# Three row norms moved into the projections behind them, and the adding of expert results joined to one of them

## The reference

```python
def rms_norm(x, g):
    xf = x.astype(jnp.float32)
    y = xf * lax.rsqrt(jnp.mean(xf * xf, axis=-1, keepdims=True) + EPS)
    return (y * g.astype(jnp.float32)).astype(x.dtype)
...
        h = rms_norm(x, attn_norm_g[l])
        proj = jnp.matmul(h, w_in[l])
...
    y = jnp.zeros_like(hf).at[row_tok].add(yb.reshape(n_rows, D))
...
        h = _rmsnorm(x, norm_mix_pre[l]).astype(dt)
        z = h @ w_in[l]
...
        h = _rmsnorm(x, norm_ffn_pre[l]).astype(dt)
        gate, up = jnp.split(h @ ffn_w_up[l], 2, axis=-1)
        gate = _causal_dwconv(gate, ffn_conv_w[l], ffn_conv_b[l])
```

## Time and profile before

| what | us |
|---|---|
| median of 3 runs | 3374.01 (3365.13 to 3382.85) |
| the profiled execution, its own time | 3364.43 |
| its span on the core | 3362.7 |
| TensorE busy | 2846.3 (85% of the span) |
| VectorE busy | 1820.1 (54%) |
| ScalarE busy | 1352.1 (40%) |
| GpSimd busy | 352.3 (10%) |
| mean granted TensorE clock | 0.908 of full speed |

### The profile page before, as it was taken

How to read it: one execution, slowest core, us unless ns; L and a number is a source line. 1 busy time by engine, 2 the same in 40 slices (tenths; PEclk the granted TensorE clock), 3 DMA queues, 4 the chain that set the end, 5 groups by cost and what they waited for, 6 DMA issues and landing times. The chain is left out here.

```text
span 3362.7 us, 43086 instructions
## 1 busy us (share of the span) xinstructions
PE 2846.3 (85%) x14395; PEld 2341.1 (70%) x14395; DVE 1820.1 (54%) x2202; ACT 1352.1 (40%) x2006; POOL 352.3 (10%) x247
## 2 busy tenths in 40 slices
PE   3999987799559999993799978178976999999997
PEld 2788776687448888882677776066855788887876
DVE  2796417663459999995262444754345233332344
ACT  3222427612248888883222133345334222222232
POOL 0222210020021111111122100001000000000000
PEclk8999998899779999996899978598677999999999
DMA  2112225132189999994212210301121211111122
GB/s 83 35 49 74 81 78 186 44 107 100 65 295 412 412 412 412 412 404 187 57 54 79 70 32 2 113 14 42 22 91 66 63 50 44 49 44 37 50 103 78
DMA packets 253206, 420.94 MB, mean 125 GB/s; under 512 B 40141, under 2 KB 157956, under 8 KB 253092
## 3 DMA queue, kind: packets, MB, share of 16 engines
q1 hardware_dynamic: 217204, 349.83, 29.2%
q10 hardware_dynamic: 26496, 39.62, 3.2%
q0 software_dynamic: 9392, 29.99, 2.6%
HBM read 349.01 MB, written 70.36 MB: 125 GB/s over the span
## 5 line engine op out<-in xcount | busy, mean ns | idle before, releaser
L1870 DVE TENSOR_TENSOR e_w_lo<-e_ring,e_w_hi 128x1024 fp32r<-128x1024 f32 x384 | 446.5, 1217 | 47.8 <-ACT e_w_hi L1797 47.8
L1797 ACT CAST e_w_hi<-e_ring 128x1024 fp32r<-128x1024 f32 x384 | 377.6, 1049 | 38.1 <-PE banks L1727 30.3
L2199 PE MATMUL banks<-h_hi,u_w_hi 128*128 128x512 f32 x704 | 274.8, 390 | 10.4 <-DVE u_w_lo L2233 10.4
L2200 PE MATMUL banks<-h_lo,u_w_hi 128*128 128x512 f32 x704 | 274.6, 390 | 0.0
L2201 PE MATMUL banks<-h_hi,u_w_lo 128*128 128x512 f32 x704 | 274.5, 390 | 0.0
L1725 PE MATMUL banks<-e_w_hi,e_xT_hi 128*128 128x512 f32 x512 | 202.8, 396 | 0.0
L1727 PE MATMUL banks<-e_w_hi,e_xT_lo 128*128 128x512 f32 x512 | 200.0, 391 | 0.0
L1726 PE MATMUL banks<-e_w_lo,e_xT_hi 128*128 128x512 f32 x512 | 199.6, 390 | 0.0
L713 DVE SCALAR_TENSOR_TENSOR conv<-x_first,vectors,conv 128x1024 f32<-128x1024 f32 x120 | 187.7, 1564 | 9.0
L563 PE MATMUL banks<-h_hi,p_w_hi 128*128 128x512 f32 x384 | 155.0, 404 | 11.8 <-POOL p_w_lo L698 11.8
L2199 PEld LDWEIGHTS banks<-h_hi,u_w_hi 128*128 128x128 f32 x704 | 132.7, 188 | 38.3 <-issue 10.8
(11 more groups left out here) (548 smaller groups left out, 6359.5 us busy)
## 6 DMA issues: line engine op xcount, KB each, us to landing
e_ring<-in_w_gate_e_dram SPq DMA_DIRECT2D x128, 512.0 KB, 8.8
e_ring<-in_w_up_e_dram SPq DMA_DIRECT2D x128, 512.0 KB, 10.6
e_ring<-in_w_down_e_dram SPq DMA_DIRECT2D x128, 512.0 KB, 8.0
yT<-in_ffn_w_up_dram SPq DMA_DIRECT2D x44, 512.0 KB, 3.9
expert_results<-nothing SPq DMA_DIRECT2D x1, 16384.0 KB, 50.3
expert_results<-e_y ACTq DMA_DIRECT2D x32, 512.0 KB, 7.9
p_w<-in_w_in_dram SPq DMA_DIRECT2D x24, 512.0 KB, 3.9
fd_w<-in_ffn_w_down_dram SPq DMA_DIRECT2D x44, 256.0 KB, 2.7
```

Source lines behind the costliest of these rows:

```text
L1797: nc.scalar.copy(w_hi[:, part, :], experts.ring[:, slot, :]).then_inc(w_rounded, 1)
L1870: tt(w_lo[:, part, :], experts.ring[:, slot, :], w_hi[:, part, :].bitcast(F32), ALU.subtract).then_inc(w_split, 1)
L2199: nc.tensor.matmul(bank, w_hi[:, up, k, :], h_hi[:, k, tokens], start=(k == 0), stop=False)
L2200: nc.tensor.matmul(bank, w_hi[:, up, k, :], h_lo[:, k, tokens], start=False, stop=False)
```

## The change

Each of the three norms now runs inside the block of the projection that reads it, as `RowNorm` (n1, n4) or `CombinedNorm` (n3).

- Every engine's program of the projection starts with the norm's part. SP loads the weights of units 0 and 1 at once; `fill` of units 0 and 1 stands between the steps of the norm on ScalarE, and in `ffn_up` the rest of the weights between those on VectorE.
- `first_units` on TensorE: turn tiles 0 to 5; when tiles 0 to 3 have their rest (`parted`), multiply half 0 of unit 0 and of unit 1, with the turning of tile 6 after 3 feature slices and of tile 7 after 6; when all tiles have their rest, half 1 of unit 0 and of unit 1. The order is unit 0 half 0, unit 1 half 0, unit 0 half 1, unit 1 half 1; before it was both halves of unit 0 and then those of unit 1.
- In `ffn_up`, `projected` is raised by 2 after all four quarters; before it was raised by 1 after each unit.
- The squares, root and reciprocal of n1 move into `load_vectors`, tile by tile as x lands.
- The gathers, the adding, the squares and the storing of x (now 8 DMAs, one a tile) move into `project_columns`. Root and reciprocal are formed for two tiles at a time. The gathers have four tile slots (in `z_rwkv`) where they had eight. The recycling and the small block with the table now come ahead of the gathers.
- `zm`, `values` and `mlstm_o` lie in the place of `x`; no DMA or operation is added by that.

The diff, cut to its core:

```diff
--- before.py
+++ after.py
@@ -216,7 +219,11 @@
             dve.drain()
             nc.vector.tensor_reduce(dots[:], prod[:], AX, ALU.add).then_inc(lam_dot, 1)
             dve.wait_ge(lam_exp, 1)
+            dve.wait_ge(squared, 1)
+            nc.vector.tensor_scalar(ss[:], ss[:], 1.0 / D, EPS, ALU.mult, ALU.add).then_inc(meaned, 1)
             nc.vector.tensor_scalar(K.lam[:], exps[:, 1:2], exps[:, 0:1], -LAM_INIT, ALU.subtract, ALU.add)
+            dve.wait_ge(rooted, 1)
+            nc.vector.reciprocal(ss[:], ss[:])
...
+            for t in range(NT):
+                act.wait_ge(x_landed[t // 4], 16)
+                nc.scalar.activation(junk[:], x[:, t, :], ACT.Square, accum_out=ss[:, t:t + 1])
+                act.drain()
             act.wait_ge(lam_dot, 1)
             nc.scalar.activation(exps[:], dots[:], ACT.Exp).then_inc(lam_exp, 1)
-    return x_landed
+            act.sem_inc(squared, 1)
+            act.wait_ge(meaned, 1)
+            nc.scalar.activation(ss[:], ss[:], ACT.Sqrt).then_inc(rooted, 1)
...
+class RowNorm:
...
+    def scale(self, act, t):
+        if t >= 2:
+            act.wait_ge(self.turned, t - 1)
+        self.K.nc.scalar.activation(self.xn[:, t % 2, :], self.x[:, t, :], ACT.Copy, scale=self.rstd[:, t:t + 1]).then_inc(self.scaled, 1)
+
+    def round_off(self, act, t):
+        act.wait_ge(self.gained, t + 1)
+        self.K.nc.scalar.activation(self.hi[:, :, t * P:(t + 1) * P], self.whole[:, t % 2], ACT.Copy).then_inc(self.rounded, 1)
+
+    def turn(self, pe, t):
+        b = t % 2
+        pe.wait_ge(self.scaled, t + 1)
+        if t >= 2:
+            pe.wait_ge(self.gained, t - 1)
+        for k in range(KT):
+            mm = self.K.nc.tensor.transpose(self.K.ps[:, 4 + 2 * b + k // 4, (k % 4) * P:(k % 4 + 1) * P],
+                                            self.xn[:, b, k * P:(k + 1) * P], self.K.const("ident"))
+        mm.then_inc(self.turned, 1)
...
+    def on_scalar(self, act, between={}):
+        self.scale(act, 0)
+        self.scale(act, 1)
+        for t in range(NT):
+            self.round_off(act, t)
+            if t + 2 < NT:
+                self.scale(act, t + 2)
+            if t in between:
+                between[t]()
...
+    def on_vector(self, dve, between={}):
+        self.times_gain(dve, 0)
+        for t in range(NT):
+            if t + 1 < NT:
+                self.times_gain(dve, t + 1)
+            self.rest(dve, t)
+            if t in between:
+                between[t]()
+
+    def first_units(self, pe, split, banks, w_hi, w_lo, projected):
+
+        mm = self.K.nc.tensor.matmul
+        for t in range(NT - 2):
+            self.turn(pe, t)
+        for h in range(2):
+            pe.wait_ge(self.parted, NT // 2 * (h + 1))
+            for u in range(2):
+                if h == 0:
+                    pe.wait_ge(split, u + 1)
+                bank, tokens = banks(u, h), slice(h * HALF, (h + 1) * HALF)
+                for k in range(KT):
+                    mm(bank, w_hi(u, k), self.hi[:, k, tokens], start=(k == 0), stop=False)
+                    mm(bank, w_hi(u, k), self.lo[:, k, tokens], start=False, stop=False)
+                    last = mm(bank, w_lo(u, k), self.hi[:, k, tokens], start=False, stop=(k == KT - 1))
+                    if h == 0 and u == 0 and k in (2, 5):
+                        self.turn(pe, NT - 2 + (k == 5))
+                last.then_inc(projected, 1)
...
+class CombinedNorm(RowNorm):
...
+    def on_gpsimd(self, pool):
+        for t in range(NT):
+            if t >= self.SLOTS:
+                pool.wait_ge(self.added, t - self.SLOTS + 1)
+            for c in range(2):
+                pool.indirect_dma_start(self.y[:, t % self.SLOTS, c, :], None, self.results,
+                                        bass.IndirectOffsetOnAxis(ap=self.dest[:, 2 * t + c:2 * t + c + 1], axis=0)) \
+                    .then_inc(self.gathered[t], 16)
+
+    def on_sync(self, sp):
+        for t in range(NT):
+            sp.wait_ge(self.added, t + 1)
+            sp.dma_start(self.keep[t * P:(t + 1) * P, :], self.x[:, t, :]).then_inc(self.x_kept, 16)
+
+    def on_scalar(self, act, between={}):
+        for q in range(NT // 2):
+            for t in (2 * q, 2 * q + 1):
+                act.wait_ge(self.added, t + 1)
+                self.K.nc.scalar.activation(self.junk, self.x[:, t, :], ACT.Square, accum_out=self.rstd[:, t:t + 1])
+                act.drain()
+            act.sem_inc(self.squared, 1)
+            if q:
+                self.round_off(act, 2 * q - 2)
+            act.wait_ge(self.meaned, q + 1)
+            self.K.nc.scalar.activation(self.rstd[:, 2 * q:2 * q + 2], self.rstd[:, 2 * q:2 * q + 2], ACT.Sqrt).then_inc(self.rooted, 1)
+            if q:
+                self.round_off(act, 2 * q - 1)
+            act.wait_ge(self.rated, q + 1)
+            self.scale(act, 2 * q)
+            self.scale(act, 2 * q + 1)
+            if q in between:
+                between[q]()
+        self.round_off(act, NT - 2)
+        self.round_off(act, NT - 1)
+
+    def add(self, dve, t):
+        dve.wait_ge(self.gathered[t], 32)
+        for c in range(2):
+            last = self.K.nc.vector.scalar_tensor_tensor(self.x[:, t, :], self.y[:, t % self.SLOTS, c, :], self.weights[:, t, c:c + 1],
+                                                         self.x[:, t, :], ALU.mult, ALU.add)
+            if c == 0:
+                dve.drain()
+        last.then_inc(self.added, 1)
...
+    def on_vector(self, dve):
+        self.add(dve, 0)
+        self.add(dve, 1)
+        self.add(dve, 2)
+        self.mean(dve, 0)
+        self.add(dve, 3)
+        self.rate(dve, 0)
+        for q in range(NT // 2):
+            t = 2 * q
+            more = t + 4 < NT
+            if more:
+                self.add(dve, t + 4)
+            if t + 2 < NT:
+                self.mean(dve, q + 1)
+            self.times_gain(dve, t)
+            self.times_gain(dve, t + 1)
+            self.rest(dve, t)
+            if more:
+                self.add(dve, t + 5)
+            if t + 2 < NT:
+                self.rate(dve, q + 1)
+            self.rest(dve, t + 1)
+        dve.wait_ge(self.x_kept, 16 * NT)
...
+            norm.on_sync(sp)
...
+            norm.first_units(pe, split, lambda u, h: K.ps[:, 2 * u + h, :], lambda u, k: w_hi[:, u, k * P:(k + 1) * P],
+                             lambda u, k: w_lo[:, u, k * P:(k + 1) * P], projected)
+            for u in range(2, U):
                 b = u % 2
                 pe.wait_ge(split, u + 1)
                 for h in range(2):
-                    pe.wait_ge(kept, 2 * u + h + 1)
+                    pe.wait_ge(kept, 2 * u + h + (2 if u == 2 and h else 1))
...
-            fill(0)
-            fill(1)
+            norm.on_scalar(act, {1: lambda: fill(0), 2: lambda: fill(1)})
+            for n, (u, h) in enumerate([(0, 0), (1, 0), (0, 1), (1, 1)]):
+                _, out, scale, func, _ = units[u]
+                act.wait_ge(projected, n + 1)
+                keep(out(h), K.ps[:, 2 * u + h, :], func, scale, None)
+                if h == 1:
+                    fill(u + 2)
...
+            norm.on_gpsimd(pool)
...
+            norm.on_scalar(act, {2: lambda: fill(0), 3: lambda: fill(1)})
...
+                if h == 1:
+                    fill(u + 2)
...
+            norm.first_units(pe, split, lambda up, h: K.ps[:, 2 * up + h, :], lambda up, k: w_hi[:, up, k, :],
+                             lambda up, k: w_lo[:, up, k, :], halves)
+            pe.wait_ge(halves, 4)
+            pe.sem_inc(projected, 2)
+            block(0, 1)
+            with pe.Fori(1, FFT // 2) as i:
                 for b in range(2):
-                    for up in range(2):
-                        pe.wait_ge(split, i * 4 + (2 * b + up + 1))
-                        pe.wait_ge(done, i * 2 + (b + 1))
-                        for h in range(2):
-                            bank, tokens = K.ps[:, 4 * b + 2 * up + h, :], slice(h * HALF, (h + 1) * HALF)
-                            for k in range(KT):
-                                nc.tensor.matmul(bank, w_hi[:, up, k, :], h_hi[:, k, tokens], start=(k == 0), stop=False)
-                                nc.tensor.matmul(bank, w_hi[:, up, k, :], h_lo[:, k, tokens], start=False, stop=False)
-                                mm = nc.tensor.matmul(bank, w_lo[:, up, k, :], h_hi[:, k, tokens], start=False, stop=(k == KT - 1))
-                        mm.then_inc(projected, 1)
+                    block(i, b)
...
-            for up in range(2):
-                fill(0, up)
+            act.wait_ge(meaned, 1)
+            nc.scalar.activation(ss[:], ss[:], ACT.Sqrt).then_inc(rooted, 1)
+            act.wait_ge(rated, 1)
+            norm.on_scalar(act, {1: lambda: fill(0, 0), 3: lambda: fill(0, 1)})
...
+            norm.on_vector(dve, {1: lambda: fill(0, 0), 3: lambda: fill(1, 1)})
...
-            z = Z["rwkv"] = K.sb(inner, "z_rwkv", [P, 8, 1 + S])
```

(10 more changed lines are left out.)

166 lines of the change are left out of this document (97 added, 69 removed).

## The result

The median after is 3328.4 us (3324.1 to 3334.5, 4 runs), beside 3371.3 (3365.1 to 3382.9, 4 runs) for the kernel before; the ratio on record is 0.9855, with a 95% interval of 0.9823 to 0.9888 (the ratios here are those on record; they are not the quotients of the medians beside them, which here would be 0.9873, inside the interval). That is 43 us by the medians and 34.7 by the two profiled executions (3364.4 and 3329.7; spans 3362.7 and 3327.3). In four later series of the kernel before (11 to 17 runs) its medians were 3369.0, 3376.7, 3376.8 and 3372.4 us, and single runs lay between 3353 and 3395.

The account below looks back on a forecast made before the run. TensorE was taken to bound the dense stages around each norm, but the tile chain the norms themselves. Gains 24.4 + 12.9 + 1.7 = 39.0 us off the median 3374.0 gave 3335, range 3325 to 3346, chance 0.70.

Parts of the forecast that it names:

- n1: Attention norm and first projection: fourth quarter done at 73.2 us against 97.57, gain 24.4, bounds 19 to 27.
- The splits: GpSimd's `w_lo` colliding with VectorE's rests: partial price, 0.6 us taken in n1; by the full rule 9.6 in all.
- the 3 us that I had named as a sign of being wrong: GpSimd's weight splits: any taking over 3 us would show the forecast wrong.
- n3: Adding of expert results and mixers' norm: fourth quarter at 1631.3 us against 1644.24, gain 12.9, bounds 3 to 19.
- stop at tile 6: TensorE inside n3's quarters: stands about 2.7 us, root and reciprocal being queued behind gains of tiles 4 and 5.
- n4: Feed-forward norm and `ffn_up`: 2635.0 us against 2636.7, gain 1.7, bounds -4 and +5.
- the cover that I had called gone: `ffn_up`: gate chain no longer hidden under the up unit, so TensorE stands 7.4 us.
- Everything behind shifts with it: All stages after each place: assumed to move with the end of its fourth quarter, no size of its own.
- (a): Rival: collisions and starved gathers; n3 gains nothing, n1 loses 4 more; gain 22, 3352 us; chance 0.13.
- (b): Rival: clock stays low through first units in all three places; 13 us slower than before, 3387; chance 0.03.
- (c): Rival: no stall at tile 6, early gathers, no clock loss; gain about 50, 3324 us; chance 0.08.
- (d): Rival: earlier start only in name, a later wait takes it back; gain 0 to 15, about 3366; chance 0.06.

Follow-up runs that it names:

- e8: Changed kernel with the last tile pairs reordered in the mixers' norm and the first weights rounded behind the squares; 3309.8 us, ratio 0.9811.
- e7: Changed kernel with feed-forward halves signalled as they come and the second tile's weights rounded and split ahead of the first filter; 3310.5 us, ratio 0.9818.
- e5: Kernel before with only unused gaps of 128 bytes a partition behind x_first and ahead of the mixers' first tile; 3360.0 us, ratio 0.9944.
- e12: Kernel before with only unused gaps, 192 bytes behind x_first and 128 ahead of the mixers' first tile; 3368.7 us, ratio 0.9977.
- e4: Changed kernel with the feed-forward norm n4 put back as a block of its own; 3310.2 us, ratio 0.9867.
- e1: The changed kernel itself, run again with nothing altered; 3320.3 us, ratio 0.9873.
- e6: Changed kernel with 44 identity turnings into an unused bank ahead of the router block's first TensorE wait; 3321.2 us, ratio 0.9851.

## Why the prediction was right, step by step

- **The whole**: 39 us forecast, 43 by the medians; 3328 against 3335, of which 3 us are the fourth run of the kernel before, which moved its median from 3374.0 to 3371.3. The sum was near partly by luck, by terms that it did not contain and that nearly cancelled: in the profiled execution the three stages gave 49 us of their own (29.3 + 15.1 + 5.0), placement about 9, the router's clock took 15.7 and smaller losses in other stages some 8 more, which leaves 35. The medians hold executions with other clocks.
- **n1: 24.4 forecast, 29.3 measured**, above my bound of 27. The mis-sized terms: the squares' spacing of 1.54 was that of a loop with 0.39 idle in each pass; written out, it is 1.22, and the first scaling came 1.7 earlier than forecast (25.86 against 27.6). From there to the first matmul 16.8, forecast 17.7. The quarters and turnings took 68.31 - 42.65 = 25.7 instead of 27.9: a turning inside dense work moved the next matmul by 0.79 (46.42 to 47.21), and I had put 1.6. The 1.6 was an estimate from the row at the low clock (1.97). The trace of before has eight turnings at the full clock too, in its router block, with the next matmul 0.91 behind their start; they would have given 1.8 for both in place of 3.2. Timeline, TensorE, before:

```profile
877.70 1.07 PE L1401 MATMUL banks<-consts,r_h 128*128 128x128 f32 x8
878.61 1.87 PE L1409 MATMUL banks<-r_w,r_h2T 128*128 128x36 f32 x16
```

- **The splits**: they did collide, 2.63 and 3.03 us, with VectorE's rests at 2.07 and 1.93 instead of 1.22. The second is just over the 3 us that I had named as a sign of being wrong. The first matmul waited for the turning of tile 5 all the same. The Trainium skill (SBUF — State Buffer, Who interferes with whom) has the two exclude each other; the times that both took agree with that, but most gathers took their 0.94 beside adds (a few of them 1.7 to 1.9), and its full price, 9.6 us, did not appear: little of the collisions lay on the path.
- **n3: 12.9 forecast, 15.1 measured** at the fourth quarter. First gather 4.6 later (4.4), first add 7.8 behind it (8), first matmul 47.6 (47.9), stop at tile 6 of 2.98 (2.7). What was over is again the turnings and the quarters, 30.6 instead of 32.6. e8 shows that the stop belonged to the order of ScalarE's and VectorE's work; with the clock around it, it was worth 6 to 8 us.
- **n4: 1.7 forecast, 5.0 measured**, at the upper bound. First matmul 17.2 after the first scaling (17.4), stop 7.63 (7.4), slow matmuls behind it some 1.8 (2.5), the quarters 24.8 instead of 27.2. e7 confirms the cover that I had called gone: put back in another way, it returned 9.7 us.
- **"Everything behind shifts with it"** is the step that failed, in both directions. Stages with unchanged code ran at another pace because their tiles had moved, and one ran at half clock. e5 and e12 show the first, e4 beside e1 the second.
- **Rivals**: (a) gathers were not starved, but the sign that I had named for it came in small: GpSimd waited 0.82 us for an add before it could use a slot again, which I had called done by then, and VectorE waited 0.77 and 2.10 us for gathers in the middle of the adds; (b) 8 to 13 of the 96 matmuls were slow in each place (n4 8, n1 10, n3 13), and then the full clock was back; (c) "all fits" was nearest in the stages; (d) had no part.

## What to carry to other kernels

When a norm is joined to the projection behind it, look at what the first units release and in which order each engine takes the last tiles: the two stops that the joining made cost 6 to 8 and about 10 us, and both went by a change of order alone. Compare stages by the lead at fixed instructions, not whole times, when the clock of one stage takes 16 us in one profiled execution and not in another. And look at the remainder of the tiles' addresses before a pace is put down to code.

## What the runs showed of the hardware that I had not expected

- A dense stage's matmul pace depends on where its tiles lie: 0.2268 to 0.2342 us a matmul of 512 columns for the same instructions, in steps that repeat to 0.0003 and change with gaps of 64 to 192 bytes. The same gap of 128 bytes made the units faster (0.2323 to 0.2300) and the slabs slower (0.2289 to 0.2333).
- A stage in which TensorE is busy without a gap ran at half clock for 40 us in eight executions and at full clock in three. Work ahead of it raised the clock, which was at half again 3 us into the block and stayed there while TensorE was busy without a gap (e6).
- Turnings alone raised the granted clock (0.92 in e6's second window), and 44 of them took 6.8 us.
